# Stick breaking: GpSimd sums the logarithms of the key blocks, TensorE multiplies the sum with ones once

## The reference

```python
def stick_breaking(q, k, v):
    """A[t,s] = sigmoid(z_ts) * prod_{s<j<t} (1 - sigmoid(z_tj)), s < t."""
...
        z = jnp.einsum('bhqd,bhkd->bhqk', qb, k).astype(jnp.float32) * scale
        log_1m = jnp.where(causal, jax.nn.log_sigmoid(-z), 0.0)
        between = lax.cumsum(log_1m, axis=3, reverse=True) - log_1m
        a = jnp.where(causal, jnp.exp(jax.nn.log_sigmoid(z) + between), 0.0)
        return jnp.einsum('bhqk,bhkd->bhqd', a.astype(v.dtype), v)
```

## Time and profile before

| | us |
|---|---|
| Median of three runs | 1414.91 (1414.4 to 1415.01) |
| The profiled execution's own time | 1415.17 |
| Its span in the trace | 1413.4 |
| PE busy | 1370.6 (97%) |
| DVE busy | 617.6 (44%) |
| ACT busy | 442.1 (31%) |
| POOL busy | 60.2 (4%) |

### The profile page before, as it was taken

How to read it: one execution, slowest core, us unless ns; L and a number is a source line. 1 busy time by engine, 2 the same in 40 slices (tenths; PEclk the granted TensorE clock), 3 DMA queues, 4 the chain that set the end, 5 groups by cost and what they waited for, 6 DMA issues and landing times.

```text
span 1413.4 us, 16272 instructions
## 1 busy us (share of the span) xinstructions
PE 1370.6 (97%) x6572; PEld 872.8 (62%) x6572; DVE 617.6 (44%) x1107; ACT 442.1 (31%) x751; POOL 60.2 (4%) x113
## 2 busy tenths in 40 slices
PE   6999999899899999999899999999999999999998
PEld 5777675675443344334333475655788888888886
DVE  5224556836343344333433565587443222233234
ACT  4125775721100110110200263476343222223232
POOL 0001120000210010000000001000000000000000
PEclk9999999999999999999999999999999999999999
DMA  8541117549999999999999822000161322313001
GB/s 353 216 181 60 60 61 317 249 149 355 387 405 422 424 426 424 426 424 422 423 425 426 313 100 81 30 1 1 60 238 60 119 86 93 119 63 117 30 1 60
DMA packets 32900, 304.13 MB, mean 215 GB/s; under 512 B 6139, under 2 KB 6331, under 8 KB 11064
## 3 DMA queue, kind: packets, MB, share of 16 engines
q1 hardware_dynamic: 30120, 298.69, 52.3%
q0 software_dynamic: 2272, 3.53, 0.7%
q10 hardware_dynamic: 432, 0.85, 0.2%
HBM read 302.62 MB, written 4.26 MB: 217 GB/s over the span
## 4 chain that ended last, share of the span: by engine, by line
PE 83%; DMA 7%; DVE 6%; issue 1%; ACT 1%; POOL 1%; DVEq 0%; ACTq 0%; SPq 0%
PE ps L58 79%; DMA ring<-in_w 3%; DMA B<-in_w 3%; PE ps L1324 2%; DMA MISC<-table 1%; PE ps L997 1%; PE ps L1041 1%; DVE LL L2025 1%; DVE TMP L2113 1%; DMA table<-MISC,SMI 1%; DMA X<-in_x 0%; POOL table L626 0%; DVE LH L2116 0%; POOL TMP L609 0%; PE ps L691 0%
## 5 line engine op out<-in xcount | busy, mean ns | idle before, releaser
L58 PE MATMUL ps<-XH,WH 128*128 128x512 f32 (+1 forms) x384 | 143.3, 373 | 1.1 <-DVE XL L2025 0.7
L58 PE MATMUL ps<-XL,WH 128*128 128x512 f32 (+1 forms) x384 | 142.6, 371 | 0.0
L58 PE MATMUL ps<-XH,WL 128*128 128x512 f32 (+1 forms) x384 | 142.6, 371 | 0.0
L58 PE MATMUL ps<-ring,B 128*64 128x512 f32 (+3 forms) x592 | 138.9, 588 | 1.3 <-DMA ring<-in_w 1.1
L58 PE MATMUL ps<-B 128*64 128x512 f32 (+5 forms) x408 | 103.0, 556 | 0.9 <-DMA B<-in_w 0.6
L1684 ACT ACTIVATE TMP<-ps,MISC 64x512 f32<-64x512 f32 x28 | 19.2, 684 | 263.0 <-PE ps L58 263.0
L2381 DVE TENSOR_TENSOR X<-ps,X 128x512 f32<-128x512 f32 x112 | 69.7, 684 | 55.2 <-PE ps L58 55.1
L58 PEld LDWEIGHTS ps<-ring,B 128*64 128x64 f32 (+1 forms) x592 | 41.5, 137 | 71.2 <-issue 66.1
L1907 ACT ACTIVATE WH<-ring 128x2048 fp32r<-128x2048 f32 x23 | 44.1, 1918 | 129.0 <-PE ps L58 129.0
L2025 DVE TENSOR_TENSOR WL<-ring,WH 128x2048 fp32r<-128x2048 f32 x23 | 52.7, 2293 | 71.2 <-ACT WH L1907 71.2
L58 PEld LDWEIGHTS ps<-XH,WH 128*128 128x128 f32 x384 | 72.3, 188 | 14.9 <-DVE XL L2025 1.9
(11 more groups left out here) (372 smaller groups left out, 2453.0 us busy)
## 6 DMA issues: line engine op xcount, KB each, us to landing
ring<-in_w SPq DMA_DIRECT2D x52, 2048.0 KB, 26.8
B<-in_w SPq DMA_DIRECT2D x28, 2048.0 KB, 24.5
ring<-in_w_ada SPq DMA_DIRECT2D x12, 2048.0 KB, 9.1
MORE<-in_w SPq DMA_DIRECT2D x10, 2048.0 KB, 23.4
ring<-in_w_gu SPq DMA_DIRECT2D x7, 2048.0 KB, 8.6
ring<-in_w_in SPq DMA_DIRECT2D x6, 2048.0 KB, 12.6
TO<-in_w SPq DMA_DIRECT2D x6, 2048.0 KB, 15.7
ring<-in_w_down SPq DMA_DIRECT2D x4, 2048.0 KB, 7.4
```

The lines of the kernel that those rows point to most:

```text
L58: return e.matmul(o, l, r, start=first, stop=last, skip_group_check=True)
```

## The change

The products of block 0 with the −1 matrix, one for each later key block, become one. For this the logarithms of blocks 1, 2 and 3 of a head are first added for each query, by POOL, into SP (384 columns in MORE, one for even and one for odd heads). POOL does it in two steps, each behind the selects of a group: for g = 2 it copies the first 128 columns of block 2 and adds block 3 to its last 128; for g = 1 it copies the first 128 columns of block 1 and adds the other 256 to the sums. DVE then splits the sums into SPH and SPL as it does LP, behind its split of g = 0, and PE multiplies SPH and SPL with −1. Blocks 1, 2 and 3 keep their products. Since LL overwrites LP, DVE's subtraction for g = 2 and g = 1 waits for POOL's sums (sb_sum) as well.

```diff
+    SP = [MORE[:, 1024 + 768 * k:1408 + 768 * k] for k in range(2)]
+    SPL, SPH = ([again(f"{n}{k}", [128, 384], "MORE", a + 768 * k) for k in range(2)] for n, a in (("SPL", 1024), ("SPH", 1408)))
...
+        def blocks_summed(i, g):
+            l, s = LP[i % 2], SP[i % 2]
+            e.wait_ge(sb_lsel, 4 * i + 4 - g)
+            if g == 2:
+                e.tensor_copy(s[:, 128:256], l[:, 896:1024]).then_inc(sb_sum, 1)
+                e.tensor_tensor(s[:, 256:384], l[:, 1024:1152], l[:, 1152:1280], ALU.add).then_inc(sb_sum, 1)
+            else:
+                e.wait_ge(sb_sum, 4 * i + 2)
+                e.tensor_copy(s[:, 0:128], l[:, 512:640]).then_inc(sb_sum, 1)
+                e.tensor_tensor(s[:, 128:384], s[:, 128:384], l[:, 640:896], ALU.add).then_inc(sb_sum, 1)
+
         for m in range(4):
             for i in (2 * m, 2 * m + 1):
                 for g in (2, 1, 0):
                     e.wait_ge(sb_relu, 3 * i + 3 - g)
                     for c in blocks[g]:
                         select(LP[i % 2][:, off[c]:off[c] + 128]).then_inc(sb_lsel, 1)
+                    if g:
+                        blocks_summed(i, g)
...
             for g in (2, 1, 0):
-                e.wait_ge(sb_split, 6 * i + 2 * (3 - g))
+                e.wait_ge(sb_split, 8 * i + 2 * (3 - g))
                 for c in blocks[g]:
                     o = place(i, c)
                     t = below(i, o, ntri, ntr, c)
-                    for d in range(c + 1, 4):
+                    if c == 0:
+                        e.wait_ge(sb_split, 8 * i + 8)
+                        mm(e, o[:, 128:512], nor, SPH[i % 2][:, :], False, True)
+                        t = mm(e, o[:, 128:512], nor, SPL[i % 2][:, :], False, True)
+                    for d in range(c + 1, 4 if c else 1):
                         t = below(i, o[:, 128 * (d - c):512 - 128 * c], none, nor, d)
...
             e.wait_ge(sb_lsel, 4 * i + 4 - g)
+            q = 8 * i + 2 * (2 - g)
             e.tensor_copy(LH[k][:, a:b], LP[k][:, a:b]).then_inc(sb_split, 1)
-            e.wait_ge(sb_split, 2 * n + 1)
+            e.wait_ge(sb_split, q + 1)
+            if g:
+                e.wait_ge(sb_sum, 4 * i + (4, 2)[g - 1])
             minus(LL[k][:, a:b], LP[k][:, a:b], LH[k][:, a:b]).then_inc(sb_split, 1)
+            if g == 0:
+                e.tensor_copy(SPH[k][:, :], SP[k]).then_inc(sb_split, 1)
+                e.wait_ge(sb_split, q + 3)
+                minus(SPL[k][:, :], SP[k], SPH[k][:, :]).then_inc(sb_split, 1)
```

More of the change, by code:

```diff
@@ L422, in body @@
     ada_mm, ada_row, ada_T, ada_mod, mod_set = (sem(n) for n in ("ada_mm", "ada_row", "ada_T", "ada_mod", "mod_set"))
-    tri_set, sb_z, sb_log, sb_relu, sb_lsel, sb_split, sb_s, sb_exp, sb_asel, sb_o, sb_oT = (
-        sem(n) for n in ("tri_set", "sb_z", "sb_log", "sb_relu", "sb_lsel", "sb_split", "sb_s", "sb_exp", "sb_asel", "sb_o", "sb_oT"))
+    tri_set, sb_z, sb_log, sb_relu, sb_lsel, sb_sum, sb_split, sb_s, sb_exp, sb_asel, sb_o, sb_oT = (
+        sem(n) for n in ("tri_set", "sb_z", "sb_log", "sb_relu", "sb_lsel", "sb_sum", "sb_split", "sb_s", "sb_exp", "sb_asel", "sb_o", "sb_oT"))
     sbn_act, sbn_mm, sbn_out, od_sq, od_rs, od_nrm, od_T, od_hi, od_lo, so_hi, so_lo = (
@@ L443, in body @@
                     tb_set, lam_dot, lam_exp, lam_set, cs_exp, cs_set, da_s, da_max, da_exp, da_w, da_q, da_r, da_T, da_wt, da_o, od_out,
-                    ada_mm, ada_row, ada_T, ada_mod, tri_set, sb_z, sb_log, sb_relu, sb_lsel, sb_split, sb_s, sb_exp,
+                    ada_mm, ada_row, ada_T, ada_mod, tri_set, sb_z, sb_log, sb_relu, sb_lsel, sb_sum, sb_split, sb_s, sb_exp,
                     sb_asel, sb_oT, sbn_act, sbn_mm, sbn_out, od_sq, od_rs, od_nrm, od_T, od_hi, od_lo, so_hi, so_lo, wo_hi, x1,
```

## The result

The changed kernel takes **1435.95 us** (median of 4 runs, 1435.33 to 1436.42), the kernel before beside it 1414.66 us (1413.84 to 1415.01, 4 runs). The ratio is 1.0152, with a 95% interval of 1.0139 to 1.0165: 21.3 us slower, where the forecast was 14.1 us. The profiled execution has a span of 1434.2 us, against 1413.4.

The account below looks back on a forecast made before the run. DVE's order, level with or ahead of PE, was taken to bound the stick-breaking stage; pair delays 3.61 + 3 x 3.49 = 14.1 us took the profiled 1415.17 to 1429.3, median 1429.0 us; range 1423.5 to 1437.0.

Parts of the forecast that it names:

- the clock rival: PE standing still in each pair lowers its granted clock; four falls add 6.8 us, giving 1435.8 us; chance 0.20.
- DVE's order is the bound through both heads: Stick-breaking stage: in all four pairs DVE's order is level with PE or ahead, so work added there goes into the time.
- the slack of 0.64: Odd head's projection, later pairs: DVE's normalization is seen at 161.96 us, 0.64 us before PE wants it at 162.60.
- The products taken from PE, costed at nothing: Key block 0: 0.46 us less on PE a head, 3.7 over eight, hidden by DVE's chain and counted as nothing.
- The wait of LL for POOL's sums, 0.55 and 0.70 us: DVE's subtraction waits for POOL's copy and add: 0.55 us more for g = 2 and 0.70 for g = 1.
- I charge POOL those 0.18 us: POOL's loss beside a DVE cast: two selects took 0.72 us against 0.54 alone; charged in each of g = 2 and g = 1.
- The port rule of the Trainium skill: POOL's copy starts only behind DVE's whole cast: terms 0.64 and 0.86 us, result some 2.0 us later than forecast.
- The split of the sums, 0.87 us: DVE casts and subtracts the sums (128x384) behind LL of g = 0: 0.39 + 0.48 = 0.87 us a head.
- The sum of a pair, 3.49 and 3.61: Odd head's projection comes 3.61 us later in the first pair, 3.49 in each of three later pairs: 14.1 us.
- From 230 us on every row is shifted alike.: Sign that the forecast is right: behind the stick-breaking stage, all rows come later by the same time.
- Absorbed later: Rival: weight loads behind the stage keep their time, giving back up to 3.9 us: 1425.1 us; chance 0.10.
- the other signs named ahead: LL waits 0.4 to 0.9 us more, odd projections start 3 to 4 later, PE's waits grow from 1 to 16 to 20.

Follow-up runs that it names:

- the run with PE fed: Changed kernel plus nine products that nobody reads, ahead of PE's waits in each odd head: 1431.3 us, ratio 1.0117.
- the version with the split elsewhere: Changed kernel with LL in MORE, ACT rounding the sums into SPH and POOL subtracting for SPL, DVE's list as before the change: 1420.35 us, ratio 1.0045.

## Why the prediction was right, and by how much it was off

The result lies in the range, at its upper part: 1435.95 in 1423.5 to 1437.0, with 0.95 given to slower. The forecast of 1429.0 was 7 us low. The range holds only because it had been stretched for the clock: with the forecast's own prices it ended at 1433.6, which is 2.4 us below the result. That the clock rival names 1435.8, almost the result, is luck: its waits were 2.5 us too small (14.1 for 16.6) and its clock 2.2 us too dear (6.8 for 4.6). Step by step:

- **DVE's order is the bound through both heads.** Right. In the second pair DVE's normalization starts 11.05 us after PE's even mark before (161.15) and 15.75 us in the changed kernel (171.74), 4.70 us later; less the slack of 0.64 this is 4.06, and the run with PE fed shows 4.09. PE waits for LL in every odd head. A stage (122 to 222 us) in which PE is busy for 99% was bound by an engine that is busy for 55%.
- **The products taken from PE, costed at nothing.** Right for the changed kernel: with 16.6 us of delay in DVE's order, no part of them shows. The run without the −1 products bounds it, if DVE does not come later: the even head's part is worth nothing but for 0.3 us in the first pair, and the odd head's at most 0.64 us a pair.
- **The wait of LL for POOL's sums, 0.55 and 0.70 us.** The mechanism was right, the size wrong: 0.63 and 0.92 us, +0.30 us a head, 2.4 us over eight. This is the term of the sum that was mis-sized. The add of 256 columns takes 0.73 us (0.60 taken), that of 128 columns 0.45 (0.38). "I charge POOL those 0.18 us" stood for what the copy loses beside a cast: measured 0.12 and 0.19, well met. So two thirds of the error are the adds, whose second operand I had priced at a memset's 0.85 ns for each element. Most of the rest is the step from the add's end to LL's start, 0.10 us where I took 0.03. From the two adds alone (0.46 and 0.73 for 128 and 256 columns) it is 2.1 ns for each element more, against the 1.7 ns that my two passes made.
- **The port rule of the Trainium skill.** With the rule of the Trainium skill, SBUF — State Buffer, section Who interferes with whom, the prediction came to 0.64 and 0.86 us. That was nearer to the measured 0.63 and 0.92 than mine, in part by chance, since it was worked out with my adds. I held against it that POOL lost less than a whole cast. That was the wrong comparison, since only an overlap can be lost. The cast starts at 160.02 us, when the first select (159.94 to 160.23) still has 0.21 us to run, and takes 0.06 us longer than alone; the second select starts at about 160.19, when the cast has 0.32 us to run, and POOL loses 0.18. Those are the overlaps less about 0.15 us, as in the places below.
- **The split of the sums, 0.87 us.** Right: LL of g = 0 at 160.74 to UL at 162.22 is 1.48 us where it was 0.61, so 0.87; in the odd head 0.95, since the cast takes 0.45 beside POOL's selects. Alone it makes 4.9 us of the time.
- **The sum of a pair, 3.49 and 3.61.** With the measured prices the same sum gives 3.49 + 2 x 0.30 = 4.09 and 4.21; the run with PE fed shows 4.09 to 4.11 and 4.30. The sum over the pairs is 16.6 us instead of 14.1.
- **Clock, a rival with a chance of 0.20.** It came, in all four pairs, on top of the forecast. The step that failed is the reading of the earlier trace rows, "1.99 of 4 us busy (704 to 708) left it at 1.00", as evidence against a fall: in the changed kernel 0.92, 0.93 and 1.08 of 2 us in a row were followed by one. One stretch that kept its clock said little: the version with the split elsewhere kept it too, with PE busy for 3.02 of 5 us (158 to 163) and waiting 1.76 us. The price was closer: 1.7 us for each fall was the estimate, 5.8 us for the four were measured at the end of the stage, 4.6 in the time. With the waits as measured and this, 1414.9 + 16.6 + 4.6 = 1436.1.
- **"From 230 us on every row is shifted alike."** Wrong. 6.0 us are gained at the routing and 3.3 are given back near 700 us. "Absorbed later", the rival, holds in part for a time and not in the result. Of the other signs named ahead, LL of g = 1 waits 0.92 us more (0.4 to 0.9 was named), the odd projection comes 4.2 to 4.4 us later (3 to 4), and PE's waits grow to 15.1 us (16 to 20).

## What to carry to other kernels

A high busy share of one engine does not say that its order is the bound: the chain over the engine that it waits for, however short the waits, decides what removed work is worth and what added work costs. When a step that another engine feeds is made to wait, look also at what lies behind the wait: idle time in front of dense products was paid twice here, once as a wait and once as a lower clock. An output that overwrites its input makes every further reader of that input a wait; moving LL elsewhere took away 13.5 of the 21.3 us.

## What the runs showed of the hardware

**DVE's casts and subtractions and POOL's instructions hold each other up almost one for one.** In six places one engine's instruction starts while the other's runs. In each the later one takes longer than alone by the overlap less about 0.14 us. The copy behind the casts of 256 and 384 columns, in the changed kernel: overlap 0.26 and 0.33 us, longer by 0.12 and 0.19. POOL's adds behind the subtraction LL, in the version with LL in MORE, where they take 0.66 and 1.08 us instead of 0.45 and 0.73:

```profile
159.54 0.66 POOL L618 TENSOR_TENSOR MORE<-TMP 128x128 f32<-128x128 f32 x1
...
161.23 1.08 POOL L622 TENSOR_TENSOR MORE<-MORE,TMP 128x256 f32<-128x256 f32 x1
```

```profile
159.46 0.43 DVE L2044 TENSOR_TENSOR LL<-TMP,LH 128x256 fp32r<-128x256 f32 x1
...
161.15 0.56 DVE L2044 TENSOR_TENSOR LL<-TMP,LH 128x384 fp32r<-128x384 f32 x1
```

Overlap 0.35 and 0.48, longer by 0.21 and 0.35. DVE behind POOL's subtraction, in the version with the split elsewhere: overlap 0.95 and 0.82, longer by 0.81 and 0.68. The cast or subtraction of DVE that started first kept its time. DVE's maximum, which reads the scores from PSUM, is not held up: at 161.62 us in the version with LL in MORE it lies wholly beside POOL's add and takes 0.68 us, as elsewhere, and the add's 0.35 us are accounted for without it. The Trainium skill, SBUF — State Buffer, section Who interferes with whom, says that whoever issues first has the shared pair for the whole instruction; the trace agrees, but for the 0.14 us. That the 0.14 us are the start of an instruction, in which it touches no memory, is argued from the numbers and was not tried.

**Short waits were enough for the clock, but their length does not decide.** No wait of PE in the stage was longer than 1.8 us in the changed kernel, and the clock fell in all four pairs; with waits of at most 1.14 us (LL in MORE) it still fell behind two of four. The pairs in which it fell there and those in which it did not look alike: PE was busy for 3.58 of 5 us in 159.7 to 164.7 (second pair, no fall) and in 185 to 190 (third pair, a fall). With the split elsewhere PE stood still for longer, 1.53 to 1.76 us ahead of g = 0, and the clock stayed at 1.00 in all four. What tips it stays open. Useless products in the waits kept it up in both versions that had them.

**A shift in time is not carried through unchanged.** The same work behind the stage took 6 us less or 3 us more, by what it met of other transfers. Why the table's read lands sooner in the changed kernel was seen only in the records of its transfer (12 and 8 us); what held it up before was not tried.
